# Prompt attention on one Trainium2 core: probabilities and values split into fp32r halves, one product per key block

## The reference

```python
q, k, v, logf, u = project(x, w_in, b_f)          # 8 heads of 64, and 4 pool groups of 128
Fh = jnp.cumsum(logf, axis=1).transpose(0, 2, 1)
s = einsum('bqhd,bkhd->bhqk', q_blk, k) * 64 ** -0.5 + (F_blk[..., :, None] - Fh[..., None, :])
s = jnp.where(kpos[None, :] <= qpos[:, None], s, NEG_INF)
out = einsum('bhqk,bkhd->bqhd', softmax(s), v)
pool = pool_mix(u, ...)                            # moving means and a 128x128 product per group
x1 = layer_norm(ALPHA * x + concat(attn, pool) @ w_o)
y = layer_norm(ALPHA * x1 + (silu(x1 @ w_gate) * (x1 @ w_up)) @ w_down)
```

## Time and profile before

| | us |
|---|---|
| runs of the kernel before | 1395.48, 1396.32, 1396.60 (median 1396.32) |
| the profiled execution, its own time | 1396.35 |
| its span, from the first to the last instruction | 1394.5 |
| TensorE busy | 1343.7 (96%) |
| VectorE busy | 693.9 (50%) |
| ACT busy | 358.6 (26%) |
| GpSimd busy | 548.5 (39%) |
| mean granted TensorE clock | 0.989 of 2.4 GHz |

### The profile page before, as it was taken

How to read it: one execution, slowest core, us unless ns; L and a number is a source line. 1 busy time by engine, 2 the same in 40 slices (tenths; PEclk the granted TensorE clock), 3 DMA queues, 4 the chain that set the end, 5 groups by cost and what they waited for, 6 DMA issues and landing times. The chain is left out here.

```text
span 1394.5 us, 21289 instructions
## 1 busy us (share of the span) xinstructions
PE 1343.7 (96%) x7605; PEld 1078.8 (77%) x7605; DVE 693.9 (50%) x1038; ACT 358.6 (26%) x527; POOL 548.5 (39%) x262
## 2 busy tenths in 40 slices
PE   7899999999989899999999999999999999999997
PEld 5889999999869886677777777777777776666675
DVE  4745665653556583553546465544634334321327
ACT  3524444443341233112021202121210201111116
POOL 1014454704110036656575657566562212121114
PEclk9999999999989999999999999999999999999999
DMA  7334453511035216777777777778776445367533
GB/s 246 104 116 150 129 185 103 170 43 53 25 107 219 86 45 220 256 243 243 231 261 240 243 247 241 234 236 266 222 253 215 158 141 202 152 262 277 223 145 122
DMA packets 111769, 255.02 MB, mean 183 GB/s; under 512 B 12848, under 2 KB 22961, under 8 KB 106280
## 3 DMA queue, kind: packets, MB, share of 16 engines
q1 hardware_dynamic: 102384, 247.00, 53.0%
q10 hardware_dynamic: 8320, 4.19, 1.1%
q0 software_dynamic: 960, 2.47, 0.5%
HBM read 243.73 MB, written 10.12 MB: 182 GB/s over the span
## 5 line engine op out<-in xcount | busy, mean ns | idle before, releaser
L829 POOL TENSOR_TENSOR WL<-WR,WH 128x1024 fp32r<-128x1024 f32 x55 | 132.1, 2402 | 427.4 <-ACT WH L1051 427.4
L769 POOL TENSOR_TENSOR AR<-AR,QB 128x1024 f32<-128x1024 f32 x96 | 232.6, 2439 | 101.1 <-DMA AR<-cache_k 88.5
L1454 PE MATMUL PSM<-XH,WH 128*128 128x512 f32 x672 | 215.7, 402 | 0.0
L1454 PE MATMUL PSM<-XL,WH 128*128 128x512 f32 x672 | 210.7, 395 | 0.0
L1454 PE MATMUL PSM<-XH,WL 128*128 128x512 f32 x672 | 210.7, 394 | 0.0
L2029 DVE TENSOR_TENSOR ACC<-ACC,PSM 128x512 f32<-128x512 f32 x160 | 108.7, 684 | 141.6 <-PE PSM L1464 141.5
L1454 PEld LDWEIGHTS PSM<-XH,WH 128*128 128x128 f32 x672 | 121.9, 188 | 53.3 <-issue 27.6
L1051 ACT CAST WH<-WR 128x1024 fp32r<-128x1024 f32 x55 | 57.5, 1047 | 367.3 <-PE PSM L1454 189.5
L1454 PEld LDWEIGHTS PSM<-XH,WL 128*128 128x128 f32 x672 | 126.3, 188 | 29.9
L1454 PEld LDWEIGHTS PSM<-XL,WH 128*128 128x128 f32 x672 | 126.2, 188 | 29.6
L1464 PE MATMUL PSM<-R 128*128 128x512 f32 x528 | 148.5, 390 | 0.1
(11 more groups left out here) (266 smaller groups left out, 2144.3 us busy)
## 6 DMA issues: line engine op xcount, KB each, us to landing
AR<-cache_v SPq DMA_DIRECT2D x256, 256.0 KB, 3.3
AR<-cache_k SPq DMA_DIRECT2D x192, 256.0 KB, 3.5
AR<-ws SPq DMA_DIRECT2D x37, 1024.0 KB, 6.4
WR<-ffn SPq DMA_DIRECT2D x66, 512.0 KB, 4.8
WR<-w_in SPq DMA_DIRECT2D x20, 512.0 KB, 4.7
ACC<-cache_k SPq DMA_DIRECT2D x32, 256.0 KB, 3.0
WR<-cache_k SPq DMA_DIRECT2D x32, 256.0 KB, 3.0
WR<-w_o SPq DMA_DIRECT2D x5, 1024.0 KB, 4.9
```

The lines of the kernel that those rows point to most:

```text
L769: pool.tensor_tensor(keys, keys, QB[:].rearrange("p (o n) -> p o n", o=1).to_broadcast([P, KP, AW]), ALU.mult).then_inc(k_mul, 1)
L829: pool.tensor_tensor(lo, WR[:, raw_weight(e), :], hi.bitcast(F32), ALU.subtract).then_inc(ffn_lo, 1)
L1454: ins = pe.matmul(out[:, hc], (hi, lo)[a][:, k * P:(k + 1) * P], x[b][:, k, hc], start=(k == 0 and n == 0), stop=(k == KC - 1 and n == 2))
```

## The change

The turned probabilities are written as two fp32r parts, high by ACT's copy, low by VectorE's subtraction, in every slot, side by side per key block (`split_rows`); even and odd slots have a buffer each, the odd one in other memory for each part of the stage. Values are split in the same way, once per pair (`VHL`: per key block and head 64 columns high, 64 low). One fp32r product per key block, with 128 columns of values as weights and 256 columns of probabilities moving, gives 128 rows by 256 columns of OB. The output now stands with head dimensions in partitions: it is the sum of rows 0 to 63 of both halves and rows 64 to 127 of the first (low times low is left unused), times the reciprocal of the row sum, which TensorE brings into the same bank by a transpose of a broadcast column. VectorE does this a slot later (`output_rows(x - 3)`), right behind its first step of the slot, in three instructions, into its final home in ACC; the turns of pairs go. The values are turned in slot 2 instead of slot 1; ACT copies them twice (high part, and rows for the store), then VectorE subtracts. The key and value rows for the stores share one buffer. There are two buffers for early keys instead of four. Memory is reassigned, and waits follow that.

Waits and context of little weight are left out of this diff, which is shown with its indentation reduced.

```diff
@@ -49,7 +49,7 @@
-KE = 4
+KE = 2
@@ -220,11 +220,17 @@
+with nc.sbuf_tensor("SPLITW", [P, WS * D], F32R) as SPLITW:
+    pass
...
+with nc.sbuf_tensor("SPLITA", [P, RT * D], F32R) as SPLITA:
+    pass
...
+with nc.sbuf_tensor("SPLIT", [P, 8 * D], F32R) as SPLIT:
+    pass
@@ -326,23 +332,35 @@
-PT = [AR[:, n * D:(n + 1) * D] for n in (2, 3)]
+def split_rows(v):
+    if v % 2 == 0:
+        home = SPLIT[:, 2 * D:4 * D]
+    elif v < SLOTS - STEPS:
+        home = SPLITA[:, 4 * D:6 * D]
+    elif v < SLOTS - RT:
+        home = SPLITW[:, D:3 * D]
+    else:
+        home = R2[:, 0:2, :].rearrange("p a n -> p (a n)")
+    return home.rearrange("p (k a n) -> p k a n", k=RT, a=2)
...
-AO = AR[:, 6 * D:7 * D]
+VHL = SPLIT[:, 6 * D:8 * D].rearrange("p (k h a n) -> p k h a n", k=RT, h=2, a=2)
...
-VN = [ACC[:, 5, :], AR[:, 7 * D:8 * D]]
+VN = KN
...
-KX = [ACC[:, 7, :], ACC[:, 4, :]]
+KX = [ACC[:, 7, :], ACC[:, 3, :]]
...
-scanmask = VN[1]
+scanmask = ACC[:, 4, :]
...
-KE_SLOTS = [ACC[:, 2, :], ACC[:, 3, :], WR[:, 2, :], WR[:, 1, :]]
+KE_SLOTS = [WR[:, 2, :], WR[:, 1, :]]
@@ -362,6 +380,8 @@
+HOME = [ACC[:, 7, :], ACC[:, 1, :], ACC[:, 2, :], ACC[:, 3, :]]
 def raw_product(n, m):
@@ -400,13 +420,12 @@
-    torder += [("vn", p)] if s == 1 and p < PAIRS else []
-    torder += [("ct", p - 1)] if s == 2 and p >= 1 else []
+    torder += [("vn", p)] if s == 2 and p < PAIRS else []
...
-T = numbered(torder + [("ct", PAIRS - 1), ("sn", 0), ("sn", 1), "un"] + [("x1", i) for i in range(RT)])
+T = numbered(torder + [("sn", 0), ("sn", 1), "un"] + [("x1", i) for i in range(RT)])
@@ -439,6 +458,7 @@
+pt_hi, vn_kept, home_done = sem("pt_hi"), sem("vn_kept"), sem("home_done")
@@ -550,13 +570,11 @@
-            early_keys(0)
-            early_keys(1)
...
-            early_keys(2)
-            early_keys(3)
+            early_keys(0)
+            early_keys(1)
@@ -600,14 +618,14 @@
+    sp.wait_ge(ob_full, O["pv", SLOTS - RT - 1] + 1)
...
-            sp.wait_ge(tb_full, T["ct", PAIRS - 1] + 1)
-            sp.wait_ge(vn_st, 16 * PAIRS)
+            sp.wait_ge(ob_full, O["pv", SLOTS - 1] + 1)
@@ -877,17 +895,18 @@
-            elif p >= 2:
+            elif p == 1:
+                act.wait_ge(tb_full, T["g", 1] + 1)
+            else:
...
+                if p == 2:
+                    act.wait_ge(home_done, 1)
...
-            if g == 0:
-                act.wait_ge(tb_full, T["kn", PAIRS - 1] + 1)
-            act.wait_ge(conv_lo, 6 * (PAIRS - 1) + (6 if g == 0 else 4) if g in (0, 2) else 6 * (PAIRS - 1))
-            if g == 1:
+            act.wait_ge(conv_lo, 6 * (PAIRS - 1) + 4 * (g == 2))
+            if g <= 1:
...
-                act.wait_ge(vn_st, 16 * (PAIRS - 1))
@@ -909,25 +928,35 @@
     def store_rows(kind, p):
-        act.wait_ge(tb_free, T[kind, p] + 1)
-        src, dst, stored = (KN, t["k_p"], kn_st) if kind == "kn" else (VN[p % 2], t["v_p"], vn_st)
+        if kind == "kn":
+            act.wait_ge(tb_free, T["kn", p] + 1)
+        else:
+            act.wait_ge(vn_kept, p + 1)
+        src, dst, stored = (KN, t["k_p"], kn_st) if kind == "kn" else (VN, t["v_p"], vn_st)
...
     def key_rows(p):
...
-            act.wait_ge(kn_st, 16 * p)
+            act.wait_ge(vn_st, 16 * p)
...
-    def keep_pair(p):
-        act.wait_ge(tb_full, T["ct", p] + 1)
-        if p == 0:
-            act.wait_ge(g_st, 16 * NB)
-        elif p == 2:
-            act.wait_ge(k_red, EARLY)
-        act.copy(ACC[:, p, :], TB).then_inc(tb_free, 1)
+    def value_rows(p):
+        act.wait_ge(tb_full, T["vn", p] + 1)
+        if p >= 1:
+            act.wait_ge(ob_full, O["pv", STEPS * p - 1] + 1)
+        act.wait_ge(kn_st, 16 * (p + 1))
+        act.copy(VHL.rearrange("p k h a n -> p (k h) a n")[:, :, 0, :], TB.rearrange("p (k n) -> p k n", n=HD))
+        act.copy(VN, TB).then_inc(vn_kept, 1)
+    def keep_home(p):
+        act.wait_ge(ob_free, O["pv", STEPS * p + STEPS - 1] + 1)
+        act.wait_ge(g_st, 16 * NB)
+        act.copy(ACC[:, p, :], HOME[p]).then_inc(home_done, 1)
...
     def output_hi(m):
@@ -943,8 +974,10 @@
     def cat_rows_hi(half, k):
...
-        if k < PAIRS:
-            act.wait_ge(tb_free, T["ct", k] + 1)
+        if k == 0:
+            act.wait_ge(home_done, 1)
+        elif k < PAIRS:
+            act.wait_ge(ob_free, O["pv", STEPS * k + STEPS - 1] + 1)
@@ -989,8 +1022,10 @@
-        if s == 2 and p >= 1:
-            keep_pair(p - 1)
+        if s == 2 and p < PAIRS:
+            value_rows(p)
+        if s == 2 and p == 1:
+            keep_home(p - 1)
@@ -1000,12 +1035,14 @@
-        if 0 <= v < SLOTS and v % 2:
-            w = (v % RT + 1) * P
+        if 0 <= v < SLOTS:
+            n = v % RT + 1
...
-            act.copy(PT[1][:, 0:w], TB[:, 0:w]).then_inc(tb_free, 1)
+            if v == SLOTS - STEPS + 1:
+                act.wait_ge(k_red, EARLY)
+            act.copy(split_rows(v)[:, 0:n, 0, :], TB[:, 0:n * P].rearrange("p (k n) -> p k n", n=P)).then_inc(pt_hi, 1)
@@ -1269,21 +1303,18 @@
     def weighted_values(v):
-        p, s = divmod(v, STEPS)
-        hh, i = s // RT, s % RT
-        ob = claim_ob(O["pv", v])
+        p, at = divmod(v, STEPS)
+        hh, i = at // RT, at % RT
+        claim_ob(O["pv", v])
+        pe.wait_ge(inv_done, v + 1)
+        pe.transpose(OB[0:HD, 2 * P:3 * P], rinv[:, i, hh:hh + 1].to_broadcast([P, HD]), ident[:])
...
-            ins = pe.matmul(ob[:, 0:HD], PT[v % 2][:, kt * P:(kt + 1) * P],
-                            VN[p % 2][:, kt * P + hh * HD:kt * P + hh * HD + HD],
-                            start=(kt == 0), stop=(kt == i))
+            ins = pe.matmul(OB[:, 0:2 * P], VHL[:, kt, hh].rearrange("p a n -> p (a n)"),
+                            split_rows(v)[:, kt].rearrange("p a n -> p (a n)"), start=(kt == 0), stop=(kt == i))
...
-    def turn_pair(p):
-        claim_tb(T["ct", p])
-        pe.wait_ge(ob_free, O["pv", STEPS * p + STEPS - 1] + 1)
-        turn(lambda i: AO[:, i * P:(i + 1) * P]).then_inc(tb_full, 1)
...
     def mixer(g):
@@ -1320,12 +1351,10 @@
-        if s == 1 and p < PAIRS:
+        if s == 2 and p < PAIRS:
...
-        if s == 2 and p >= 1:
-            turn_pair(p - 1)
@@ -1736,6 +1764,25 @@
+    def output_rows(v):
+        q, r = divmod(v, STEPS)
+        hh, i = r // RT, r % RT
+        rows, dims = slice(i * P, (i + 1) * P), slice(64 * hh, 64 * hh + HD)
+        dve.wait_ge(ob_full, O["pv", v] + 1)
+        if v == 0:
+            dve.wait_ge(conv_lo, 6)
+            dve.wait_ge(tb_free, T["kn", 0] + 1)
+        elif r == 0 and q == 1:
+            dve.wait_ge(g_st, 16 * NB)
+        elif r == 0 and q == PAIRS - 1:
+            dve.wait_ge(conv_lo, 6 * PAIRS)
+            dve.wait_ge(tb_full, T["kn", PAIRS - 1] + 1)
+        out = HOME[q][dims, rows]
+        link(dve.tensor_reduce(out, OB[0:HD, 0:2 * P].rearrange("p (a n) -> p n a", a=2), AX.X, ALU.add))
+        link(dve.tensor_tensor(out, out, OB[HD:P, 0:P], ALU.add))
+        dve.tensor_tensor(out, out, OB[0:HD, 2 * P:3 * P], ALU.mult).then_inc(ob_free, 1)
@@ -1756,6 +1803,8 @@
+        if x >= 3:
+            output_rows(x - 3)
@@ -1776,38 +1825,26 @@
-        if s == 1 and p < PAIRS:
-            dve.wait_ge(tb_full, T["vn", p] + 1)
-            if p >= 2:
-                dve.wait_ge(vn_st, 16 * (p - 1))
-            dve.tensor_copy(VN[p % 2], TB).then_inc(tb_free, 1)
+        if s == 2 and p < PAIRS:
+            dve.wait_ge(vn_kept, p + 1)
+            parts = VHL.rearrange("p k h a n -> p (k h) a n")
+            dve.tensor_tensor(parts[:, :, 1, :], TB.rearrange("p (k n) -> p k n", n=HD),
+                              parts[:, :, 0, :].bitcast(F32), ALU.subtract).then_inc(tb_free, 1)
...
-            if v % 2 == 0:
-                w = (v % RT + 1) * P
-                dve.wait_ge(tb_full, T["t", v] + 1)
-                if v >= 2:
-                    dve.wait_ge(ob_full, O["pv", v - 2] + 1)
-                dve.tensor_copy(PT[0][:, 0:w], TB[:, 0:w]).then_inc(tb_free, 1)
+            q, r = divmod(v, STEPS)
+            hh, i = r // RT, r % RT
+            dve.wait_ge(pt_hi, v + 1)
+            part = split_rows(v)
+            dve.tensor_tensor(part[:, 0:i + 1, 1, :], TB[:, 0:(i + 1) * P].rearrange("p (k n) -> p k n", n=P),
+                              part[:, 0:i + 1, 0, :].bitcast(F32), ALU.subtract).then_inc(tb_free, 1)
...
-            if v >= 2:
-                dve.wait_ge(ob_free, O["pv", v - 2] + 1)
-            dve.reciprocal(rinv[:, v % 2:v % 2 + 1], rsum[:, v % 2:v % 2 + 1]).then_inc(inv_done, 1)
+            dve.reciprocal(rinv[:, i, hh:hh + 1], rsum[:, v % 2:v % 2 + 1]).then_inc(inv_done, 1)
...
-        v = x - 2
-        if v >= 0:
-            q, r = divmod(v, STEPS)
-            hh, i = r // RT, r % RT
-            dve.wait_ge(ob_full, O["pv", v] + 1)
-            dve.wait_ge(inv_done, v + 1)
-            if r == 0 and q >= 1:
-                dve.wait_ge(tb_full, T["ct", q - 1] + 1)
```

(18 more changed lines are left out.)

1 line of the change is left out of this document (removed).

## The result

The changed kernel takes 1417.43 us (median; 1414.26 to 1422.93), the kernel before beside it 1396.26 (1395.48 to 1396.60): a ratio of 1.0158, 95% interval 1.0131 to 1.0185. It is 21 us slower; forecast were 1395 us and a range up to 1408. The profiled execution took 1417.88 us, with a span of 1416.1.

The account below looks back on a forecast made before the run. TensorE, working 96% of the span, was taken as the bound. Credit 30.6 less 10.4 (values), 17 (VectorE and key buffers) and 1.5 (ACT) gave 1.7 us gained: 1395 us, range 1382 to 1408.

Parts of the forecast that it names:

- The value stall: Slot 2 of each pair: TensorE's next turn waits for VectorE's value subtraction, 2.6 us four times, -10.4 us.
- the price of two buffers: Key sets 6 to 14, pair 1: reductions take 30.5 us instead of 25.4, so VectorE falls 7 us behind.
- the round of 7.2 us: One early key buffer from reduction to next reduction: issue 0.17, landing 3.35, GpSimd's product 2.39, reduction 1.2 us.
- The term "-17": VectorE's lateness in the stage, key buffers and own work: 4, 7, 5 and 1 us lost in pairs 0 to 3.
- The slower rival: Slots 19 to 31 and 35 to 47: costlier outputs (1410) or a round of 8.7 us (1405); taken as 1406, chance 0.22.
- there is no slack: Weighted sum of slot x-2 waits for output x-3, ready 2.1 to 2.3 us after the scores; TensorE arrives at about 2.1.
- the weighted sums: TensorE's 288 products at 0.12 instead of 0.208 us: 25.3 us gained, less 6.4 for 64 transposes of the reciprocals.
- VectorE keeps up: Rival: loads land while VectorE is busy and TensorE has more slack; 12 of the 17 us stay, 1383 us, chance 0.25.
- The clock rival: New TensorE stalls of 2.6 us lower the granted clock, one stall in each pair: +5, 1400 us, chance 0.07.
- Forecast credit and debts without keys: TensorE's credit of 30.6 us, against 10.4 for the values' slot and 1.5 for ACT's chain from scores to subtraction.
- the first scan's wait: TensorE's 1.0 us wait behind VectorE's first scan goes, since VectorE has 1.2 us less before it.

Follow-up runs that it names:

- e4: Changed kernel with only the first two early key sets loaded and VectorE zeroing 16 score elements instead of each key reduction: 1397.65 us, ratio 1.0008.
- e3: Changed kernel with the loads of key sets 2 to 31 left out, products and reductions kept: 1398.82 us, ratio 1.0019.
- e5: Changed kernel with the 32 early key sets spread evenly over slots 8 to 46, never two in one slot: 1405.25 us, ratio 1.0065.
- e9: e5 with values first copied to SBUF by ACT, and low parts of the next pair's queries and keys made by GpSimd instead of VectorE: 1387.48 us, ratio 0.9936.
- e10: e9 with the outputs of slots 2 to 6 computed at the slot's end, two slots after their scores: 1383.12 us, ratio 0.9901.

## Why the prediction was wrong

**What held.** That TensorE's time is what counts at the end, and that the question was the order of VectorE's queue, not its sum. (That TensorE sets the pace held for the kernel before; in pair 1 of the changed one it works 69.2 us of 85.3.) The value stall: 2.6 us a time and 10.4 in all forecast, 2.6 at the longest and 9.8 measured. The output: 1.0 us forecast for three instructions, 0.41 + 0.29 + 0.28 measured,

```profile
L1782 DVE TENSOR_REDUCE ACC<-PSM 64x128 f32<-64x256 f32 x64 | 26.5, 414 | 2.6 <-PE PSM L1315 1.8
...
L1783 DVE TENSOR_TENSOR ACC<-ACC,PSM 64x128 f32<-64x128 f32 x64 | 18.6, 291 | 2.2
L1784 DVE TENSOR_TENSOR ACC<-ACC,PSM 64x128 f32<-64x128 f32 x64 | 18.0, 281 | 2.2
```

VectorE in pair 1: 64 us forecast, 62.5 measured. Pair 3: 3 us shorter forecast, 3.6 measured. The end was to be 2.5 us shorter; from slot 63 to the first output product it is 1.5 (25.5 to 24.1).

**The first step that failed: the price of two buffers, and the round of 7.2 us under it.** The term "-17" held key buffers and VectorE's own work; the expectation of e4 puts some 5 of it on outputs without keys, which leaves about 12 for the keys. Their loads cost 18.6 us (e3), with the reductions 19.8 (e4), so the term was some 8 us too small. Pair 1 alone is 10.6 us longer than in e3, where 7 had been forecast for loads and VectorE's work together.

Set 8's round (slots 20 and 21) was 8.7 us, because the landing took 4.9 where the prediction had 3.35. A round is counted here from the end of the reduction of set n-2 to the end of that of set n. Of the eight waits in which VectorE's 20.4 us lie, four end rounds of 7.1 to 7.6 us (sets 2, 15, 21 and 26), three end rounds of 8.7 to 9.1 (sets 8, 13 and 27), whose data took 4.7 to 5.2 us to land, and one is set 16's, which waited 3.1 us where 1 was forecast. So 7.2 was right for the shortest round and wrong as the only one. The trace of the kernel before had the spread: its 32 sets land 3.2 to 5.6 us after their issue, 14 of them after 3.9 or more, and the set right behind the one that was read, issued at 188.28 us, after 5.0. What the other transfers under way did to it is not settled by any run; the row that was used had a 512 KB load issued 0.9 us behind it, and landed fast.

Nor is the round the whole price: set 21 had one of 7.3 us, and VectorE still waited 2.75 us. e5 shows what it hangs on: 12 of the 19 us on how the sets stand, five slots with two sets. The prediction went through the sets one by one and did not ask what two sets in one slot do to a ring of two. The slower rival named a round of 8.7; that it is set 8's to the tenth is luck, since the rival came to 1406 and the kernel takes 1417. At 0.22 it stood too low, because I had the number but treated it as a risk beside one measured row.

**The second step that failed, and the larger one without keys: "there is no slack", with no price for it.** The prediction saw that the weighted sum of slot x-2 now waits for output x-3, compared 2.1 to 2.3 us with 2.1, and wrote down next to nothing for it outside the key slots. With no keys at all that wait is 11.7 us in 17 places (e4). 7.6 us of it are eight waits where splits of the next queries and keys stand ahead of the output in VectorE's queue (slots 12 and 13 of each pair, 17, 33), and 2.8 us are two behind slot 63, where the last weighted sums follow each other with nothing in between. Nor had I followed the output bank to its other users: the decoding queries wait 3.8 us for it, in slots 3 and 5, and the first scan's product, whose wait of 1.0 us I had counted as gone, waits 1.3. e9 takes the splits away (9.2 us), and outputs at the end of slots 2 to 6 take away most of the queries' wait (e10, 4.4 more, the clock's part in it).

**A term that was too small on the good side: the weighted sums.** In the changed kernel, at full clock, a sum of five products and one of eight, each with what follows it:

```profile
190.37 0.83 PE L1315 MATMUL PSM<-SPLIT 128*128 128x256 f32 x5
191.03 1.08 PE L1298 MATMUL PSM<-R 128*128 128x512 f32 x4
...
206.10 1.18 PE L1315 MATMUL PSM<-SPLITA,SPLIT 128*128 128x256 f32 x8
207.12 0.51 PE L1298 MATMUL PSM<-R 128*128 128x384 f32 x2
```

They take 0.66 and 1.02 us: 0.12 for each product, as forecast, and some 0.06 once a sum, behind the transpose. In slots 52 to 57 of pair 3, which hold sums of 3 to 8 products and no wait of TensorE in front of them, the changed kernel is 0.22, 0.31, 0.42, 0.52, 0.62 and 0.72 us shorter, where the forecast's prices (0.088 a product, less 0.1 for the transpose) give 0.16 to 0.60. Over the stage that is an estimated 4 to 5 us more than the 25.3 - 6.4 booked. So the products did not cause the miss; their gain went into waits.

**Rivals.** "VectorE keeps up" was wrong for the reason that the prediction itself held against it, the order of its queue; on average it has the time, and in e10, with 734.5 us of work, it nearly keeps up. The clock rival is real but small in the changed kernel: after the idle 3.50 us at 183.31 the products of the weighted sum in slot 21 are 0.25 us apart on average, twice what they are at full clock,

```profile
185.31 1.19 PE L1315 MATMUL PSM<-SPLITA,SPLIT 128*128 128x256 f32 x4
186.31 1.70 PE L1298 MATMUL PSM<-R 128*128 128x512 f32 x4
```

while over the pairs the granted clock is 0.98, 0.98, 1.00 and 0.98 (before 0.96, 1.00 and, in pair 3, 1.00). 0.02 of a pair is under 2 us. It adds to the stalls; no run here takes the clock's part by itself.

**The sum against the result.** Forecast credit and debts without keys come to about -13 us (30.6 less 10.4, 1.5 and the 5 for outputs); e4 measures +1.5. To the gap of 14.5 come the 4 to 5 us that the sums gave beyond the forecast. The output bank makes 10.5 of it (11.7 + 3.8, less the 5), the first scan's wait 1.3. Some 7 us stay open. A part can be the clock: from 57 to 440 us its mean is 0.96 in e4 and 0.97 in the kernel before, which is an estimated 4 us, and no run isolates it. With the loads, 20 us on top.

## What to carry to other kernels

A move of work from the bound engine to one that is half idle is paid for in the order of that engine's queue: for each instruction that frees a shared bank, list what can stand ahead of it in every slot, and look for a third engine that can take those. When a ring of buffers is cut, redo its round with the slow landings of the trace and not with one row, and look at the slots that use it twice, since spacing the uses can be worth more than a buffer. And a wait of the helper engine is no cost until someone behind it in the queue is late: going from four buffers to two cost 5 us where VectorE had room, and the loads of the two-buffer ring cost 19 where outputs and splits stood behind them. (The changed kernel with four buffers was not run.)
